# A hybrid decoder step on one core: expert weights in 2 MB transfers, two final states moved into the expert phase, and a tail by quarters of the output columns

## The reference, cut to what matters

```python
def step(S, inp):                        # retention, per chunk
    qb, kb, vb = inp
    scores = jnp.einsum('bhqd,bhkd->bhqk', qb, kb) * decay_mask
    intra = jnp.einsum('bhqk,bhkv->bhqv', scores, vb)
    cross = jnp.einsum('bhqd,bhdv->bhqv', qb * q_decay, S)
    S_new = chunk_decay * S + jnp.einsum('bhkd,bhkv->bhdv', kb * k_decay, vb)
    return S_new, intra + cross

def expert_ffn(xb, w1, b1, w2, b2):      # w1 (1024, 2048), w2 (1024, 1024), float32
    h = xb @ w1 + b1
    gate, up = h[:, :D_FF], h[:, D_FF:]
    gate = jnp.minimum(gate, SWIGLU_LIMIT)
    up = jnp.clip(up, -SWIGLU_LIMIT, SWIGLU_LIMIT)
    glu = gate * jax.nn.sigmoid(SWIGLU_ALPHA * gate)
    return ((up + 1.0) * glu) @ w2 + b2

# layer: h = x + mixer(rmsnorm(x)); h = h + moe(rmsnorm(h)); y = rmsnorm(h, norm_f)
```

## Time and profile before

| what | us |
|---|---|
| median of 3 runs | 1416.67 (1416.41 to 1417.35) |
| the profiled execution's own time | 1416.43 |
| its span | 1414.6 |
| PE busy | 1348.2 (95%) |
| DMA issues of the experts' weights: 4 MB ones | 78 |
| time in them to landing, those into the ring | 27.9 |

### The profile page before, as it was taken

The page is one execution under the profiler, slowest core; times in us unless marked ns, Lnnn a source line. Parts: engine busy times, 40 slices in busy tenths (PEclk is TensorE's granted clock), DMA queues, the critical chain, the costliest instruction groups (busy, mean ns, idle before and its releaser), DMA issues.

```text
span 1414.6 us, 17229 instructions
## 1 busy us (share of the span) xinstructions
PE 1348.2 (95%) x7181; PEld 701.9 (50%) x7181; DVE 387.4 (27%) x712; ACT 252.1 (18%) x375; POOL 95.8 (7%) x166
## 2 busy tenths in 40 slices
PE   8999999999999999999988989989999898998997
PEld 6667678888887443443333433323333342332332
DVE  4235443642501422222211211113211132121223
ACT  1233343320000421111111111011110111101112
POOL 1122212210000210000000000000000000000000
PEclk9999999999999999999999999999999999999999
DMA  9888879874524699999999999999999999999996
GB/s 351 345 302 306 300 263 343 309 280 145 188 94 185 254 415 429 430 431 431 430 431 430 433 431 432 435 433 432 430 430 433 431 432 434 433 433 429 425 428 278
DMA packets 44467, 519.95 MB, mean 368 GB/s; under 512 B 5338, under 2 KB 5898, under 8 KB 22884
## 3 DMA queue, kind: packets, MB, share of 16 engines
q1 hardware_dynamic: 29984, 470.59, 79.2%
q0 software_dynamic: 12896, 45.70, 9.4%
q10 hardware_dynamic: 1540, 2.99, 0.6%
HBM read 497.63 MB, written 21.67 MB: 367 GB/s over the span
## 4 chain that ended last, share of the span: by engine, by line
PE 68%; DMA 27%; DVE 3%; issue 1%; SPq 1%; ACT 1%; POOL 0%; DVEq 0%; POOLq 0%; ACTq 0%
PE bank L1941 25%; DMA ring<-in_w_pairs 25%; PE bank L1602 19%; PE bank L1901 4%; PE bank L1650 4%; PE bank L1993 3%; PE bank L1887 3%; PE bank L1747 2%; DMA arena<-in_state_ret 2%; PE bank L1619 1%; PE bank L1939 1%; SPq L678 1%; PE bank L1897 1%; PE bank L1970 1%; PE bank L1653 1%
## 5 line engine op out<-in xcount | busy, mean ns | idle before, releaser
L1941 PE MATMUL bank<-ring,arena 128*64 128x512 f32 x1536 | 351.9, 609 | 29.4 <-DMA ring<-in_w_pairs 29.4
L1602 PE MATMUL bank<-arena,ring 128*128 128x264 f32 x1472 | 331.5, 387 | 0.4 <-DVE arena L1193 0.4
L1602 PEld LDWEIGHTS bank<-arena,ring 128*128 128x128 f32 x1472 | 278.7, 190 | 51.0 <-issue 3.1
L1941 PEld LDWEIGHTS bank<-ring,arena 128*64 128x64 f32 x1536 | 111.2, 140 | 248.4 <-issue 230.4
L1993 PE MATMUL bank<-ring,arena 128*64 128x512 f32 x768 | 171.8, 594 | 6.2 <-DMA ring<-in_w_pairs 6.1
L1941 PE MATMUL bank<-arena 128*64 128x512 f32 x512 | 118.2, 616 | 12.2 <-DMA arena<-in_w_pairs 12.2
L1993 PEld LDWEIGHTS bank<-ring,arena 128*64 128x64 f32 x768 | 55.1, 137 | 109.0 <-issue 99.4
L1528 DVE TENSOR_SCALAR arena<-bank 128x512 f32<-128x512 f32 x32 | 22.1, 691 | 272.5 <-PE bank L1941 272.5
L1941 PEld LDWEIGHTS bank<-arena 128*64 128x64 f32 x512 | 36.9, 141 | 85.3 <-issue 68.5
L1551 DVE COPY arena<-bank 64x512 f32<-64x512 f32 x32 | 21.9, 683 | 181.3 <-PE bank L1993 181.3
L1518 DVE TENSOR_TENSOR hs<-hs,bank 128x256 f32<-128x256 f32 x16 | 6.7, 421 | 222.1 <-PE bank L1897 222.1
(11 more groups left out here) (253 smaller groups left out, 993.1 us busy)
## 6 DMA issues: line engine op xcount, KB each, us to landing
ring<-in_w_pairs SPq DMA_DIRECT2D x58, 4096.0 KB, 27.9
arena<-in_w_pairs SPq DMA_DIRECT2D x20, 4096.0 KB, 29.3
ring<-in_w_mixer SPq DMA_DIRECT2D x58, 1024.0 KB, 9.0
ring<-in_w_pairs SPq DMA_DIRECT2D x26, 2048.0 KB, 13.2
arena<-in_state_ret POOLq DMA_DIRECT2D x32, 512.0 KB, 8.1
out_ret_sample<-arena POOLq DMA_DIRECT2D x32, 512.0 KB, 6.0
arena<-in_w_pairs SPq DMA_DIRECT2D x6, 2048.0 KB, 14.5
arena<-v_decode POOLq DMA_DIRECT2D x32, 256.0 KB, 6.8
```

The source lines that it names most:

```text
L1602: ins = pe.matmul(bank[:, 0:T], weight(n + k // 4, k % 4)[:, 128 * j:128 * (j + 1)], rhs[:, k, :], start=k == 0, stop=k == KD * groups - 1)
L1941: ins = pe.matmul(out, xgT[:, k, 64 * e:64 * (e + 1)], held(n, 2 * D * (k % W1_KS) + c), start=False, stop=k == KD - 1)
```

## The change

1. `is_wide` answers False: pairs 2 to 14 are loaded in transfers of 2 MB, 156 in place of 78 of 4 MB.
2. The events `st` of heads 0 and 1, and their `kt`, leave the mixer. Each of the two heads has a `save` instead: its values, and once both heads' keys as they stand, go to DRAM (1.5 MB; the two stores of states, 1 MB, leave the mixer). `STEP_EVERY` becomes 5.0 and `VALUES_TO_STEP` 14.0, values alternate between two buffers, and at the end the planner places two closing events at a time.
3. After pair 3's loads SP issues `load_end`: the 704 KB of the tail's constants, and the kept keys and values (1.5 MB), into the spare places and others. In pair 4 PE turns the keys (8 transposes), ACT scales them, PE makes the two states (16 instructions) and ACT copies them. SP stores them (1 MB) behind the last weights.
4. The w2 of pair 15's second expert is laid out by quarters of the output columns. In `last_columns` PE finishes 128 + 128 columns at a time over all rows of w2; copies, combine, adds and squares of the first three quarters are placed before the end of the fourth. Both of pair 15's w2 (four chunks, two before) are loaded in pieces of 512 KB.
5. y_sample is stored last, by four issues, where it was stored first.

```diff
 def is_wide(pair):
-    return SPARE_PAIRS <= pair < PAIRS - 1
+    return False
...
-STEP_EVERY = 6.2
+LATE = (0, 1)
+LATE_PAIR = 4
+STEP_EVERY = 5.0
-VALUES_TO_STEP = 18.0
+VALUES_TO_STEP = 14.0
...
-        main.append((("save", h), 0.0) if h in DEFERRED else (("st", h), 3.6))
+        main.append((("save", h), 0.0))
...
-        if ends:
-            order.append(ends.pop(0))
+        for _ in range(2 if n == H * NS else 1):
+            if ends:
+                order.append(ends.pop(0))
...
-        values = [v_sb, v_sb, v_sb, view(14000, 2, DV)]
+        values = [v_sb, view(14000, 2, DV)] * 2
...
-                    if number == PAIRS - 1 and n >= PAIR_CHUNKS - W2_CHUNKS:
+                    if number == PAIRS - 1 and n >= PAIR_CHUNKS - 2 * W2_CHUNKS:
...
+            def load_end(it):
+
+                used(it, PAIR_CHUNKS - 1)
+                sp.dma_start(same_row, a["tail"][:, 0:128]).then_inc(end_in, 16)
+                sp.dma_start(nfs, a["tail"][:, 128:384]).then_inc(end_in, 16)
+                sp.dma_start(nfb, a["norm_f"].rearrange("(o n) -> o n", o=1).to_broadcast([128, D])).then_inc(end_in, 16)
+                sp.wait_ge(saved, SAVED)
+                for i in range(len(LATE)):
+                    sp.dma_start(k_late[i], k_late_dram[:, 2 * i:2 * i + 2, :]).then_inc(end_in, 16)
+                    sp.dma_start(v_late[i], v_late_dram[i]).then_inc(end_in, 16)
...
             def load_rest(r):
-                for pair in range(1, 4):
+                for pair in range(1, LATE_PAIR):
                     load_pair(r * PAIRS + pair, pair, pair)
+                load_end(r * PAIRS + SPARE_PAIRS - 1)
...
-            sp.wait_ge(up_done, 2 * PAIRS * rounds)
-            sp.dma_start(slots[0][:, 0:384], a["tail"]).then_inc(tail_in, 16)
...
+                def last_columns():
+
+                    for q in range(QUARTERS):
+                        n = PAIR_CHUNKS - W2_CHUNKS + q // 2
...
+                        for f in range(KD):
...
+                            lhs = actT[:, 1, 128 * (f % 4) + 64 * (f // 4):128 * (f % 4) + 64 * (f // 4) + 64]
+                            for side in range(2):
+                                at = 2 * D * (q % 2) + 256 * f + 128 * side
+                                ins = pe.matmul(psum[QUARTER_BANKS[q]][64 * side:64 * (side + 1), 128 * q:128 * (q + 1)], lhs,
+                                                slots[slot_of(number, n)][:, at:at + 128], start=False, stop=f == KD - 1)
+                        ins.then_inc((quarter_done, chunk_used, quarter_done, down_done)[q], 1)
+                        if q in (1, 2):
+                            combine_quarter(q - 1)
+                    combine_quarter(2)
...
+                    combine_quarter(3)
...
+                def late_states(i):
+
+                    pe.wait_ge(kept_read, 2 * len(DEFERRED) + len(LATE) + 2 * i + LATE_READS * r)
+                    for g in range(2):
+                        for t in range(2):
+                            ins = pe.matmul(psum[g][:, :], k_late[i][:, t, 128 * g:128 * (g + 1)], v_late[i][:, t, :],
+                                            start=t == 0, stop=t == 1)
+                        ins.then_inc(late_done, 1)
...
                 first_layer(1, range(4, KD))
+                if late:
+                    turn_late()
                 second_layer(0, range(0, 4))
+                if late:
+                    late_states(0)
                 turn_acts(1)
                 second_layer(0, range(4, KD))
-                second_layer(1, range(0, KD))
+                if late:
+                    late_states(1)
+                if last:
+                    last_columns()
+                else:
+                    second_layer(1, range(0, KD))
```

More of the change, by code:

```diff
@@ L936, in _ @@
                     ac.dma_start(k_kept_dram[i], ktok[:, :, :]).then_inc(saved, 16)
-                elif what == "st":
-                    for g in range(2):
-                        use = ("st", h, g)
-                        bank = read(ac, use)
-                        if g == 0 and h >= 1:
-                            ac.wait_ge(st_out, 16 * h)
-                        empties(ac.activation(st[:, g, :], bank[:, :], ACT.Copy), use)
-                    for g in range(2):
-                        was_read(ac, ("st", h, g))
-                    ac.dma_start(o["ret_prompt"][0, 0, h].rearrange("(k p) v -> p k v", p=128), st[:, :, :]).then_inc(st_out, 16)
                 elif what == "sqr":
@@ L1105, in _ @@
-            ac.wait_ge(inv3, 2)
-            ac.wait_ge(gained, 1)
-            ac.activation(y_gained, y_gained, ACT.Copy, scale=stat[:, 11:12]).then_inc(y_last, 1)
-            ac.wait_ge(y_last, 1)
-            ac.dma_start(o["y_prompt"][0, 128:256, 512:D], y_gained).then_inc(y_out, 16)
+                        if late and e == 0:
+                            late_states(1)
+                    if not last:
+                        return
+                    for q in range(QUARTERS):
+                        quarter_is_done(ac, r, it, q)
+                        ac.activation(ysb[64:128, 512 + 128 * q:512 + 128 * (q + 1)], psum[QUARTER_BANKS[q]][64:128, 128 * q:128 * (q + 1)],
+                                      ACT.Copy).then_inc(quarter_hi if q < QUARTERS - 1 else y_hi_ready, 1)
+                        if q in (1, 2):
+                            for t in range(2):
+                                ac.wait_ge(quarter_added, 4 * r + 2 * (q - 1) + t + 1)
+                                square(t, q - 1)
@@ new lines, in expert_pair @@
+                    for t in range(2):
+                        ac.wait_ge(added, ADDS * it + ADDS + t + 1)
+                        square(t, 2)
+                with ac.Fori(0, LATE_PAIR) as pair:
+                    expert_pair(pair)
+                expert_pair(LATE_PAIR, late=True)
+                with ac.Fori(LATE_PAIR + 1, PAIRS - 1) as pair:
+                    expert_pair(pair)
+                expert_pair(PAIRS - 1, last=True)
+            ac.wait_ge(added, ADDS * PAIRS * rounds + 3)
@@ new lines, in _ @@
+            ac.activation(squares3[:, 4, :], hs[:, :], ACT.Square, accum_out=stat[:, 4:5]).then_inc(hs_squared, 1)
+            for t in range(2):
+                ac.wait_ge(added, ADDS * PAIRS * rounds + t + 4)
+                square(t, QUARTERS - 1)
+                ac.wait_ge(mean3, rounds)
+                ac.wait_ge(quarter_squared, SQUARES * rounds + (SQUARES + t + 1))
+                ac.activation(stat[:, 8 + t:9 + t], sums3[:, t, LAST_SUM:LAST_SUM + 1], ACT.Sqrt,
+                              bias=sums3[:, t, REST_SUM:REST_SUM + 1]).then_inc(root3, 1)
@@ new lines, in _ @@
+            ac.wait_ge(hs_summed, 1)
+            ac.activation(stat[:, 7:8], psum[3][:, 0:1], ACT.Sqrt, scale=1.0 / D, bias=stat[:, 15:16]).then_inc(hs_root, 1)
+            for t in range(2):
+                ac.wait_ge(gained, 2 * t + 2)
+                ac.wait_ge(inv3, t + 1)
+                ac.activation(by_quarter[:, t, :, 0:2, :], by_quarter[:, t, :, 0:2, :], ACT.Copy,
+                              scale=stat[:, 10 + t:11 + t]).then_inc(y_last, 1)
+            ac.wait_ge(y_last, 2)
+            ac.dma_start(y_by_quarter[:, :, 0:2, :], by_quarter[:, 1, :, 0:2, :]).then_inc(y_out, 16)
@@ L1537, in activate, with expert_pair @@
                 v.tensor_tensor(acts, ucl, sig, ALU.mult).then_inc(act_ready, 1)
-            def expert_pair(r, pair, first=False):
+            def expert_pair(r, pair, first=False, last=False):
                 it = r * PAIRS + pair
@@ L1692, in _ @@
                         fills(ins, ("out", h, g))
-                elif what == "st":
-                    h = which[0]
-                    was_read(pe, ("kt", h))
-                    for g in range(2):
-                        bank = fill(pe, ("st", h, g))
-                        for t in range(2):
-                            ins = pe.matmul(bank[:, :], ktok[:, t, 128 * g:128 * (g + 1)], values[h][:, t, :], start=t == 0, stop=t == 1)
-                        fills(ins, ("st", h, g))
                 elif what == "step":
```

266 lines of the change are left out of this document (193 added, 73 removed).

## The result

The kernel after takes 1425.33 us in the median of five executions (1421.84 to 1425.75), the kernel before 1416.74 beside it (1416.41 to 1417.68): ratio 1.0047, 95% interval 1.0034 to 1.0061. It is slower, by half a per cent. On another chip it took 1423.43 (six executions, 1419.86 to 1426.50), ratio 1.0043 (1.0029 to 1.0057). The executions of before lie within 1.5 us of their median but for a few; those of after are spread over 3.9 us on the first chip and 6.6 us on the second.

A forecast was written before the change was run, and what follows sets the result against it. PE's work bounds the mixer, then one saturated stream of transfers sets the end. Terms -7.5 + 7.3 + 5.6 + 0.4 - 1.7 = +4.1 us gave a median of about 1420.8 us, range 1415.5 to 1425.5.

The forecast's parts named there:

- likeliest case: The forecast sum itself, chance 0.50, with its own range of 1418.3 to 1423.5 us.
- rival 3: Mixer: late loads make the state steps bind, 4 to 7.5 us of gain lost, 1424.5 to 1428; chance 0.12.
- Mixer, -7.5: Mixer: PE's removed work shortens it, less 0.5 us of new stall; -7.5 us (-8.1 to -4).
- Stream: 2 MB transfers, +7.3: Experts: two 2 MB transfers cost 0.093 us more than one of 4 MB, 78 times; +7.3 us (+5.1 to +9.9).
- rival 2: Pairs 2 to 14: 2 MB transfers cost no more than half of a 4 MB one, 1413.5 us; chance 0.12.
- Stream: what is put in, +5.6: After pair 3's loads: the 2240 KB of load_end lengthen the full stream by 5.6 us.
- The 0.4 for more pieces: Pair 15: loading two more chunks in pieces of 512 KB lengthens the stream by 0.4 us.
- Pair 4, 0: Pair 4: PE's 7.9 us of added work costs nothing, with about 28 us of transfers queued ahead.
- Tail, -1.7: Behind the last piece: quarters and reordered stores shorten the end by 1.7 us (-4 to +1).
- Rival 1: Tail: quicker quarter instructions and y's stores no longer last give back 5 us, 1417.5 us; chance 0.20.

The follow-up runs named there:

- a1: The kernel after, unchanged, run again on another chip: 1423.43 us, ratio 1.0043 to the kernel before.
- a4: The kernel after with only the first half of each sample's final state stored: 1419.25 us.
- c2: The kernel after without the store of head 1's values; pair 4 loads head 0's values twice instead: 1422.74 us, ratio 1.0046 to the kernel before.
- b3: The kernel after with head 0's closing events rsT, sqr and ss placed one event of work later: 1421.32 us.
- d1: The same kernel as b3, run once more for another profile: 1420.38 us.
- a2: The kernel after with transfers of 4 MB again in pairs 2 to 14: 1420.30 us, ratio 1.0022 to the kernel before.
- a3: The kernel before with transfers of 2 MB throughout and nothing else changed: 1422.44 us, ratio 1.0041 to the kernel before.
- b1: The kernel after with the tail's 704 KB of constants issued behind the last weights, as in the kernel before: 1423.29 us.
- b2: The kernel after with the 16 matmuls of the two late states in pair 4 done twice: 1422.70 us.
- b4: The kernel before with only the last w2 by quarters, its tail and y_sample stored last: 1414.59 us, ratio 0.9985 to the kernel before.

## Why the prediction was right, and where it was off

**Direction and range.** Slower was forecast with 0.58; 1425.33 is within the range but at its upper edge, 4.5 us above the forecast, and above the likeliest case's own range (1418.3 to 1423.5). a1 on another chip is 2.6 us above the forecast. That the number lies within the range is in part luck: it is 0.2 us from the edge, one of the five executions (1425.75) is beyond it, and 1425.33 lies where rival 3 has its own range (1424.5 to 1428).

**Mixer, -7.5: this is the term that failed.** The profiles of after gave -4.4 and -0.1. PE's own saving was there: in a4, c2, b3 and d1 chunk 5 comes at 481.3 to 481.9, 6.3 to 6.9 us sooner than before. What was mis-sized is the stall from closer state steps, put at 0.5 us: PE waited 4.1 us in one place in a1, 1.1 in the profile of after. A second part was not in the sum at all: behind the long wait the clock fell to 0.50 for 3.4 us, which cost another 1.7 us. The prediction had all the parts: loads of 8.1 us that at times take 12.8, and ACT's 41.7 us of waits for them. It looked only at `step` as the place where PE meets a late state, with 6.7 us of slack. It missed that DVE keeps one order, in which a copy that PE needs stands directly behind a state. Rival 3 had the cause and nearly the size (4 to 7.5 of the gain lost), at a chance of 0.12. That the states' transfers are behind it is shown by a4; that the 512 KB stores alone are, is not borne out by c2.

**Stream: 2 MB transfers, +7.3.** Right in sign, too large: +4.7 (a2) and +5.8 (a3) in S. Of its two stretches the first, 4.896 us, gives 5.1, and a3's medians give 5.7. The second, 4.927 us, lies in an unrolled pair, as rival 2 had noted, and one of its seven landings comes 5.2 us after the one ahead of it, with a fetched packet of code beside it. That the price is lower in the kernel after, by its landings in `arena`, no row could tell.

The Trainium skill ("DMA: Bandwidth & Descriptors", section "Anatomy of one DMA — SWDGE (gpsimd) path") puts the semaphore's write at about one cycle on trn2. The traces agree that it is next to nothing: a packet of 4 bytes and 9 ns. The page doesn't say that cutting a transfer is free; that was the prediction's own conclusion, and the runs decide against it: here the cut halves the rows of the weights too (a3).

**Stream: what is put in, +5.6.** Right: the landings show 5.6. Of these b1's landings put 1.7 on the constants, by their bytes, and leave 3.9 for the kept keys and values. The 0.4 for more pieces was not needed: the pieces land behind the last landing that PE waits for.

**Pair 4, 0.** Right, and b2 shows how much room was left.

**Tail, -1.7.** From the last landing to the span's end 13.65 us where it was 14.8: -1.15 in the profile of after. By the last landing that PE waits for it is 58.3 in place of 59.5, -1.2, in after as in b4. The instructions were priced rightly (1.75 us a quarter, forecast 1.8; 10.7 us from PE's end on, forecast 11.0). The term is off by a slip in its own sum: 9.3 us of work that starts 6.4 us ahead of the landing ends 2.9 us behind it, not 2.1, and 2.97 was measured. With 2.9 the term would have been -0.9. Rival 1 (5 us) falls.

**The sum.** In S: 7.3 + 5.6 + 0.4 - 1.7 = 11.6 was forecast, 10.0 measured. From the parts: a3's 5.8 and the 5.6 of `load_end`, less b4's 2.4, make 9.0. The landing behind chunk 5's comes 13.4 us after chunk 5's issue in after and 12.1 before, which is the 1.0 that is left and a little more; why, no run shows. So S came out 1.6 us shorter and the mixer 3 to 7 us longer than forecast: two errors that in part cancel.

## What to carry to other kernels

Read a moved step's cover (the time by which it may be late) from every engine that goes by the same order, not only from the one whose time you count: look for the copy that stands behind the late instruction. If executions vary, find a mark in the trace that splits the varying part from the rest, and price edits on the rest. Sort landings by where they go before two kernels are compared. And when a stream is the bound, whatever is moved under it is paid in full by its bytes: the saving elsewhere has to be larger, in the long executions too.

## What the runs showed of the hardware that was not expected

Two transfers of 2 MB cost 0.060 to 0.074 us more than one of 4 MB while the DMA engines show the same share busy. The second transfer's ending packet takes 9 ns of that; the rest goes with rows of 16 KB in place of 32 KB (613 ns each against 1216). Landings of 2 MB into one part of the memory come 4.85 us apart in some kernels and 4.90 in others, with the same weights and the same slots in the program.

At `load_end` SP's issues, mostly 0.3 to 0.4 us long, take up to 4.25 us, and the second behind it 8.1; among the last pieces one takes 11.1 us. So SP itself is held in places where it issues many transfers close together.

After a wait of 4.1 us PE's granted clock was 0.50 for 3.4 us and cost 1.7 us (a1); after one of 3.8 us at the same place it stayed at 1.00 (a2). And a kernel whose transfers compete in one stretch (states, their stores, kept values) spreads its executions over 6.6 us, where nearly all of the kernel before lie within 1.5 us of their median.
